# Moving the gate chunk, spreading the layer-norm statistics and regrouping the last branch gates in a two-layer encoder step

## The chip, the cores and the metric

The kernel runs on one core of a Trainium2 chip. The metric is the device time of one execution in microseconds. TensorE is called PE in the profile, VectorE DVE, ScalarE ACT, GpSimd POOL, SyncE SP.

## The reference

The model step has DEPTH = 2 layers over 512 prompt tokens and 64 sample tokens (576 columns together), D_MODEL 1024. What matters here is the first half of a layer:

```python
h = rms_norm(x, p['g_pre_mix']) * (1 + sc1) + sh1
mq, mk, mv, mo, mi, mf, su, sv, wq, wk, wv, gl = split_in(h @ p['w_in'])
ig = mi + b_igate;  lf = log_sigmoid(mf + b_fgate)          # 4 heads each: the gate rows
h_ml = mlstm_scan(q, k, v, ig, lf)                          # cumulative sums and maxima of lf, ig
y_ml = sigmoid(mo) * h_ml
y_sg, v_norm = spatial_gating(su, sv, ln_v_g, ln_v_b, ...)  # layer_norm(sv), then 128x128 mixing
y_sw = swa_prompt(rope(wq), rope(wk), wv, sinks)            # windowed attention
gates = sigmoid(gl).reshape(B, S, 3, D_MODEL)
merged = gates[0]*(y_ml @ w_br_mlstm) + gates[1]*(y_sg @ w_br_gmlp) + gates[2]*(y_sw @ w_br_swa)
x = x + g1 * rms_norm(merged @ p['w_out'], p['g_post_mix'])
```

A SwiGLU feed-forward part (hidden 2816) follows; the change leaves it alone.

## The kernel before

**Arithmetic and weights.** Activations lie with the features on the partitions and the 576 tokens in the free dimension. Each fp32 operand of a projection is split into a high part and a remainder (`h_hi`, `h_lo`; for a weight `hi`, `lo`), and three products are summed: hi·hi, hi·lo, lo·hi. A chunk is 128 output features: 8 k-tiles x 3 products x 2 halves of 288 columns = 48 matmuls (`feature_group`, L759; `main` calls it). SP loads a weight chunk into one of two RAW buffers (`load`, L576), POOL splits it with two instructions (`split`, L711 and L714) into one of two slots, of up to five where memory is free, PE uses it. All are numbered by position in the layer (P_QK = 0, ...), and each engine walks its own list of instructions, written out by hand, with semaphores between them. `carry` (L527) is a leading dummy (on PE a tiny matmul) that carries a wait.

**PSUM.** There are four units of two banks. Which unit a result gets follows from its place in the list ORDER, modulo four: a group may start once the group four places before it has been read (`empty`, `read`).

**Start of a layer.** `stream` takes the first chunks together, k-tile by k-tile, as `h_hi` and `h_lo` come (qk0 to qk2 in layer 0, qk0 to qk3 in layer 1); then come the remaining chunks up to qk7, then `wvif`, the token-major chunk of wv and the gate columns (L826, 120 matmuls of 136 columns), then `wk`. In layer 0 parts of the adaLN modulation stand between the chunks: `mod(0, a)` (L891, 64 PE instructions each), for which SP loads 2 MB of w_ada once the modulation two before it has freed its buffer (`ada_after`, L564); ScalarE copies it (L1402), PE transposes it back (`mback`, L900), VectorE takes it over (L1721).

**The gate rows.** After wk, PE transposes the gate columns into rows (`gt1`, L964, and `gt2`, L969). VectorE copies them (L1916 to L1920), and a chain of operations on 4 partitions x 576 follows, alternating between VectorE and ScalarE: -|f| (L1923), Exp and Ln (L1440, L1442), log-sigmoid (L1925), two cumulative sums (L1928), maxima (L1933, L1934), and last exponentials (L1444 to L1447, the last one writes `win` and sets `rows_ready`). PE meanwhile computes chunk v0 and then waits for `rows_ready` before `gt3` (L1062, L1064); v1 comes next.

**Attention slots and layer norm.** Ten attention slots are spread between the chunks sv0 to sv3 and the first branch. In slot i, PE does the output of slot i-2, the transposes of i-1 (L1168) and the scores of i (L1151); VectorE does `sw_max` (L2101 and after), then, for i = 4, `ln_stats` as the `between` work: bn_stats and bn_aggr of five token tiles (L2157, L2160) and two additions (L2162, L2163); then `sw_norm` once ScalarE's exponentials (L1561, L1563) are there, whose last multiplication writes `sm`. `ln_root` follows slot 5's merges; `ln_apply(t)` is the between work of slots 7 to 11. ScalarE takes the root between slots 5 and 6.

**Branches and merge.** For each branch b and each pair n of output tiles there are two gate chunks `g{b}_{n}` (ScalarE: tanh into TS) and one weight chunk for two branch groups `br{b}_{n}` of 24 matmuls each. VectorE merges (L2187 for b = 0; L2190 into WQ, then L1698 into MID for b = 1 and 2). After the last merge ScalarE writes `h_hi` of the eight tiles (L1631) and VectorE `h_lo` (L2222), and `stream` (L804 for the products with h_hi, L810 for those with h_lo) takes wo0 and wo1 together in the order k = 0 to 7. `p1` post-tiles follow.

Of the kernel before, what the change touches and what calls it, by code (L numbers as in the profile page):

```python
# [15 lines left out]
DEPTH, D, SEQ, DSEQ, PAST = 2, 1024, 512, 64, 128  # L16
# [27 lines left out]
def constants():  # L44
# [22 lines left out]
    for h in range(4):  # L67
# [16 lines left out]
AFTER = {0: {"qk3": (0, (5,), (4,)), "qk4": (0, (6,), (5,)), "qk5": (0, (7,), (6,)), "qk6": (0, (8,), (7,)),  # L84
# [28 lines left out]
def qk_order(l):  # L113
    out = [f"qk{i}" for i in range(STREAM[l])] + ([mod(0, 4)] if l == 0 else [])
    for i in range(STREAM[l], 8):
        out += [f"qk{i}"] + after(l, f"qk{i}")
    return out
# [11 lines left out]
MIX += ["gt1", "gt2", "v0", "gt3", "v1", "vt0", "kt0", "v2", "vt1", "cm0", "kt1", "v3", "vt2",  # L129
# [40 lines left out]
MIX += with_squares("wo", "p1")  # L170


def ffn_order(l):
    lm, (a, b) = IN_P1[l]
    out = [mod(lm, a), "p1s", "p1t", mod(lm, b), "p1b", "n2b"]
    for c, nb in enumerate(BLOCKS):
        for i in range(2 * nb):
            out += [f"fi{c}_{i}"] + after(l, f"fi{c}_{i}")
        if c == 1 and l == 0:
# [6 lines left out]
         for n in start_order(l) + qk_order(l) + ["wvif"] + after(l, "wvif") + ["wk"] + after(l, "wk") + MIX  # L186
# [6 lines left out]
P_QK, P_WVIF, P_WK, P_V, P_MO, P_WQ, P_SU, P_SV, P_BR = 0, 8, 9, 10, 14, 18, 22, 26, 30  # L193
# [7 lines left out]
CHUNK_OF.update({f"qk{i}": i for i in range(8)})  # L201
# [4 lines left out]
for _b_ in range(3):  # L206
    for _n in range(8):
        _p = P_BR + 12 * _b_ + 3 * (_n // 2)
        CHUNK_OF[f"g{_b_}_{_n}"] = _p + _n % 2
        if _n % 2:  # L210
            CHUNK_OF[f"br{_b_}_{_n}"] = _p + 2
CHUNK_OF.update({f"wo{i}": P_WO + i for i in range(8)})
# [58 lines left out]
def build(nc, A, O):  # L271
# [4 lines left out]
    with ctx:  # L276
# [176 lines left out]
        hl_ready = event("hl_ready", 24)  # L453
        nabs_ready = event("nabs_ready", 1)
# [96 lines left out]
        def _(sp):  # L551
# [6 lines left out]
            for l in range(DEPTH):  # L558
# [56 lines left out]
                if l == 0:  # L615
# [8 lines left out]
                    for i in range(5, 8):  # L624
                        cols(i % 2, i, w_in, i * 128)
                        ada_after(0, i + 1, i - 1)
                else:
                    for i in range(8):
                        cols(i % 2, i, w_in, i * 128)
# [3 lines left out]
                if l == 0:  # L633
                    ada_after(0, 9, 7)
                cols(1, P_WK, w_in, C_WK)
# [7 lines left out]
                for b, (nm, g, _) in enumerate(BRANCHES):  # L643
                    w_br = A[{"ml": "w_br_mlstm", "sg": "w_br_gmlp", "sw": "w_br_swa"}[nm]][ds(l, 1)] \
                        .rearrange("l (k p) c -> p (l k) c", p=128)
                    for q in range(0, 2):
                        for e in range(6):
# [3 lines left out]
                            else:  # L651
                                load(e % 2, pos, RAW[e % 2][:, 0:1024].rearrange("p (k c) -> p k c", k=4),
                                     w_br[:, :, ds(q * 512 + e // 3 * 256, 256)])
                w_out = A["w_out"][ds(l, 1)].rearrange("l (k p) c -> p (l k) c", p=128)
# [67 lines left out]
        def _(pe):  # L722
# [14 lines left out]
            for l in range(DEPTH):  # L737
# [56 lines left out]
                def stream(names, pos, ready, between=None):  # L794

                    for k in range(8):
# [1512 lines left out]
```

## Time and profile before

| what | value |
|---|---|
| three runs | 2290.62, 2290.75, 2292.04 us; median 2290.75 |
| profiled execution | 2293.98 us, its span 2292.2 us, mean granted PE clock 0.961 |
| PE, PEld busy | 2161.1 us (94%), 2080.6 us (91%) |
| DVE, ACT, POOL busy | 726.1 us (32%), 398.7 us (17%), 1237.5 us (54%) |
| DMA | 211 MB, mean 92 GB/s; the SP queue 31.9% of 16 engines' span |

The span is the time from the first to the last instruction of the profiled execution. Busy shares are averages over stages. "Released by" or "waited for" names what ended an idle stretch. PEclk is the granted TensorE clock as a share of 2.4 GHz. All times of a view are microseconds from the start of the span.

### The profile page before, as it was taken

To read this page: it belongs to the slowest core of one execution; us is meant where nothing else is said; L and a number is where in the kernel's file an instruction comes from. 1 tells how busy PE (TensorE), PEld (TensorE's weight loads), DVE (VectorE), ACT (ScalarE), POOL (GpSimd) and SP (SyncE) were. 2 spreads that over 40 slices of the span, in tenths; PEclk is the share of its full clock that TensorE was granted. 3 is DMA by queue.
4 is the path that set the end of the run, shared out by engine and by line. 5 is a ranking of instruction groups with operands and counts; after the bars stand their busy time and mean duration, and the time that the engine had idled before them with its cause. 6 is when DMAs were issued, how large, how long until landed. Compare 5 with 4: busy or idle time off the path is not lost.

```text
span 2292.2 us, 38070 instructions
## 1 busy us (share of the span) xinstructions
PE 2161.1 (94%) x16861; PEld 2080.6 (91%) x16861; DVE 726.1 (32%) x1201; ACT 398.7 (17%) x880; POOL 1237.5 (54%) x604
## 2 busy tenths in 40 slices
PE   4989999999999999999989799999999999999996
PEld 3889898999998999999989798989998899999996
DVE  4322366523255110011450335662324531001113
ACT  1211114211132110011221111330102211001111
POOL 2343353567762665666734444446686347667762
PEclk7899999999998999999979899999999899999998
DMA  8653421123342442442322152212233212222221
GB/s 267 227 166 38 65 75 56 56 77 92 93 157 64 148 145 71 125 148 75 92 56 56 47 65 62 69 47 76 76 100 127 77 49 81 73 84 83 81 76 60
DMA packets 319684, 211.05 MB, mean 92 GB/s; under 512 B 12528, under 2 KB 292512, under 8 KB 319392
## 3 DMA queue, kind: packets, MB, share of 16 engines
q1 hardware_dynamic: 312928, 205.13, 31.9%
q10 hardware_dynamic: 6592, 3.48, 0.6%
q8 instruction: 133, 2.18, 0.4%
q14 instruction: 31, 0.25, 0.0%
HBM read 203.80 MB, written 4.07 MB: 91 GB/s over the span
## 4 chain that ended last, share of the span: by engine, by line
PE 88%; DVE 5%; POOL 3%; ACT 1%; issue 1%; ACTq 1%; DMA 0%; SPq 0%; DVEq 0%; POOLq 0%
PE ps L759 59%; PE ps L784 10%; PE ps L804 4%; PE ps L891 2%; PE ps L810 2%; POOL lo L714 2%; POOL hi L711 1%; PE ps L844 1%; PE ps L826 1%; PE ps L1151 1%; PE ps L1022 1%; PE ps L1168 1%; PE ps L1192 1%; DVE h_lo L2222 1%; PE ps L1037 1%
## 5 line engine op out<-in xcount | busy, mean ns | idle before, releaser
L711 POOL TENSOR_TENSOR hi<-raw,consts 128x1024 fp32r<-128x1024 f32 (+3 forms) x260 | 467.2, 1797 | 902.8 <-PE ps L759 598.5
L714 POOL TENSOR_TENSOR lo<-raw,hi 128x1024 fp32r<-128x1024 f32 (+3 forms) x260 | 606.6, 2333 | 20.4
L759 PE MATMUL ps<-h_hi,hi 128*128 128x288 f32 x2720 | 591.0, 299 | 0.7 <-issue 0.7
L759 PE MATMUL ps<-h_hi,lo 128*128 128x288 f32 x2720 | 583.3, 296 | 0.0
L759 PE MATMUL ps<-h_lo,hi 128*128 128x288 f32 x2720 | 583.3, 296 | 0.0
L759 PEld LDWEIGHTS ps<-h_hi,hi 128*128 128x128 f32 x2720 | 438.3, 189 | 7.3 <-issue 5.3
L759 PEld LDWEIGHTS ps<-h_lo,hi 128*128 128x128 f32 x2720 | 439.3, 189 | 0.9 <-issue 0.9
L759 PEld LDWEIGHTS ps<-h_hi,lo 128*128 128x128 f32 x2720 | 439.3, 189 | 0.0
L1698 DVE TENSOR_TENSOR tmp<-sq,ps 128x576 f32<-128x576 f32 x44 | 33.1, 753 | 595.5 <-PE ps L759 573.3
L784 PE MATMUL ps<-y_hi,hi 128*128 128x288 f32 x616 | 134.7, 300 | 10.7 <-POOL lo L714 9.5
L784 PE MATMUL ps<-y_hi,lo 128*128 128x288 f32 x616 | 132.2, 296 | 0.0
L784 PE MATMUL ps<-y_lo,hi 128*128 128x288 f32 x616 | 132.0, 296 | 0.0
L1435 ACT ACTIVATE tmp<-ps 128x576 f32<-128x576 f32 x64 | 41.6, 650 | 414.5 <-PE ps L759 414.5
L784 PEld LDWEIGHTS ps<-y_hi,hi 128*128 128x128 f32 x616 | 98.7, 189 | 16.1 <-POOL lo L714 14.1
L784 PEld LDWEIGHTS ps<-y_hi,lo 128*128 128x128 f32 x616 | 99.4, 189 | 0.0
L784 PEld LDWEIGHTS ps<-y_lo,hi 128*128 128x128 f32 x616 | 99.4, 189 | 0.0
L711 POOL TENSOR_TENSOR hx<-raw,consts 128x1024 fp32r<-128x1024 f32 x29 | 55.9, 1929 | 39.6 <-DMA raw<-in_w_ffn_in 21.6
L1651 ACT ACTIVATE y_hi<-tmp 128x576 fp32r<-128x576 f32 x44 | 30.2, 686 | 267.6 <-DVE tmp L1698 267.6
L714 POOL TENSOR_TENSOR lx<-raw,hx 128x1024 fp32r<-128x1024 f32 x29 | 71.7, 2471 | 2.3
L759 PE MATMUL ps<-y_hi,hi 128*128 128x288 f32 x320 | 70.7, 303 | 0.0
L759 PE MATMUL ps<-h_hi,hx 128*128 128x288 f32 x320 | 69.4, 298 | 0.8 <-DVE ps L1798 0.8
L759 PE MATMUL ps<-y_lo,hi 128*128 128x288 f32 x320 | 68.9, 297 | 0.0
(313 smaller groups left out, 2891.2 us busy)
## 6 DMA issues: line engine op xcount, KB each, us to landing
raw<-in_w_in SPq DMA_DIRECT2D x108, 512.0 KB
ada<-in_w_ada SPq DMA_DIRECT2D x24, 2048.0 KB, 8.6
raw<-in_w_ffn_in SPq DMA_DIRECT2D x88, 512.0 KB
raw<-in_w_ffn_out SPq DMA_DIRECT2D x32, 384.0 KB
raw<-in_w_ffn_out SPq DMA_DIRECT2D x32, 320.0 KB
raw<-in_w_out SPq DMA_DIRECT2D x16, 512.0 KB
raw<-in_w_br_mlstm SPq DMA_DIRECT2D x8, 512.0 KB
raw<-in_w_br_swa SPq DMA_DIRECT2D x8, 512.0 KB
```

Source lines behind the costliest of these rows:

```text
L711: pool.tensor_tensor(hi, RAW[s][:, 0:size], ONES[:, 0:1].to_broadcast([128, size]), ALU.mult).then_inc(chunk_hi, 1)
L714: pool.tensor_tensor(lo, RAW[s][:, 0:size], hi.bitcast(f32), ALU.subtract).then_inc(chunk_split, 1)
L759: m = pe.matmul(o[:, h, :], a[:, k, c0:c0 + 128], mv(k, h), start=(k == 0 and begins), stop=(k == nk - 1 and a is wl))
L784: m = pe.matmul(o[:, h, :], a[:, k - k0, :], mv(k, h), start=(k == 0 and begins), stop=(k == nb - 1 and a is wl))
L804: pe.matmul(halves(l, nm)[:, h, :], a[:, k, :], HM[0](k, h), start=(k == 0 and a is wh), stop=False)
L810: m = pe.matmul(halves(l, nm)[:, h, :], wh[:, k, :], HM[1](k, h), start=False, stop=(k == 7))
L826: m = pe.matmul(unit(l, name)[:, c:c + w], st[:, k * T + t * 128:k * T + t * 128 + 128], mv[:, k, :], start=(k == 0 and begins), stop=(k = ...
L844: m = pe.matmul(unit(l, name)[:, c + t:c + t + 1], sq[:, t0:t0 + 128], ONES[:, 0:1], start=(begins and t == 0), stop=ends, skip_group_chec ...
L891: m = pe.matmul(unit(l, nm)[32 * x:32 * x + 32, 0:128], CS[:, k, :], wv[:, k, x * 128:(x + 1) * 128], start=(k == 0), stop=(k == 7))
L1435: act.activation(split2(dst), halves(l, name), func, scale=scale).then_inc(unit_of(l, name), 1)
L1651: act.activation(y_tile(False, i), TS[:, e, :], ACT.Copy).then_inc(gh_ready, 1)
L1698: return dve.tensor_tensor(out, a, b, op)
```

## The change

1. **Gate chunk.** `wvif` takes position 6, right behind qk5; qk6, qk7 and wk follow at 7, 8, 9. The gate transposes gt1 and gt2 stand right behind it, ahead of qk6, and wait for a new semaphore `if_ready`, set by VectorE once the gate columns have their bias; VectorE copies wv afterwards. In layer 0 the modulation parts keep their order. ScalarE copies qk6 and qk7 between the Ln and the last exponentials, and wk behind them. VectorE reads the modulation parts that belong to qk6, qk7 and wk after the gate chain.
2. **Statistics.** Tiles 0 and 1 in slot 4, tiles 2 and 3 in slot 5, tile 4 and the two additions in slot 6, the root in slot 7, `ln_apply(t)` in slot 8 + t. ScalarE's root stands after slot 6.
3. **Last gates and merged tiles.** g2_4 to g2_7 are computed together, then br2_4 to br2_7. Merges of branches 1 and 2 are made in place in PSUM, then added into MID (tiles 0 to 3 of branch 2, and branch 1) or left in PSUM (tiles 4 to 7 of branch 2). The tanh of g2_6 and g2_7 goes into SQ. The merged tiles are split and streamed in the order 0, 4, 1, 5, 2, 6, 3, 7; a PSUM unit of tiles 4 to 7 is free when its `h_lo` is made.

```diff
-    for i in range(STREAM[l], 8):
+        if i == 6:
+            out += ["wvif"] + after(l, "wvif") + ["gt1", "gt2"]
...
+        if (_b_, _n) == (2, 4):
+            MIX += [f"g2_{_i}" for _i in range(4, 8)] + [f"br2_{_i}" for _i in range(4, 8)]
+            break
...
+MERGED = (0, 4, 1, 5, 2, 6, 3, 7)
-P_QK, P_WVIF, P_WK, P_V, P_MO, P_WQ, P_SU, P_SV, P_BR = 0, 8, 9, 10, 14, 18, 22, 26, 30
+P_QK, P_WVIF, P_WK, P_V, P_MO, P_WQ, P_SU, P_SV, P_BR = 0, 6, 9, 10, 14, 18, 22, 26, 30
...
+                def gate_rows():
+                    pe.wait_ge(unit_of(l, "gt1"), empty(l, "gt1"))
+                    pe.wait_ge(if_ready, nth(if_ready, l))
...
                 for i in range(n, 8):
+                    if i == 6:
+                        pe.wait_ge(chunk_split, split_count(l, P_WVIF))
+                        token_group("wvif", P_WVIF, 136)
+                        parts_after("wvif")
+                        gate_rows()
+                        run_begins(nm, CHUNK_OF[nm])
+                    feature_group(nm, CHUNK_OF[nm], 8, 128, 0, *HM, lead=True)
...
+                for n in range(4, 8):
+                    main(f"g2_{n}", CHUNK_OF[f"g2_{n}"])
+                for n in (4, 6):
+                    branch(2, n, CHUNK_OF[f"br2_{n + 1}"])
+                stream(["wo0", "wo1"], P_WO, 8, order=MERGED)
...
+                for i in range(6):
+                    projected(i)
                 modulation_tiles("wvif")
-                tile("wk", KA[:, 0:T])
                 act.wait_ge(nabs_ready, nth(nabs_ready, l))
                 act.activation(LFT, WR, ACT.Exp).then_inc(act_step, step())
                 act.wait_ge(act_step, step.all())
                 act.activation(WR, LFT, ACT.Ln, bias=1.0).then_inc(sp_ready, 1)
+                projected(6)
+                projected(7)
                 act.wait_ge(m_ready, nth(m_ready, l))
...
+                tile("wk", KA[:, 0:T])
...
                 for n in range(8):
-                    act.wait_ge(merged2, before(merged2, l, n))
-                    tile(f"g2_{n}", TS[:, n % 2, :], ACT.Tanh, 0.5)
+                    if n < 6:
+                        act.wait_ge(merged2, before(merged2, l, n))
+                    tile(f"g2_{n}", TS[:, n % 2, :] if n < 6 else SQ[:, n - 6, :], ACT.Tanh, 0.5)
-                for k in range(8):
+                for k in MERGED:
                     act.wait_ge(merged2, nth(merged2, l, k))
+                    act.activation(split2(cols(HH, k)), split2(MID[:, k, :]) if k < 4 else halves(l, f"br2_{k}"),
+                                   ACT.Copy, scale=0.5).then_inc(hh_ready, 1)
...
+                for t0, t1, o in tiles:
                     m = tt(IFT[:, t0:t1, :], o[:, :, 128:136], BIF[:, :].unsqueeze(1).to_broadcast([128, t1 - t0, 8]),
                            ALU.add)
+                m.then_inc(if_ready, 1)
+                for t0, t1, o in tiles:
+                    m = dve.tensor_copy(VSW[:, t0:t1, :], o[:, :, 0:128])
...
-                    w = WQ[:, n % 2, :]
-                    dve.scalar_tensor_tensor(split2(w), s, 1.0, halves(l, nm), ALU.add, ALU.mult).then_inc(unit_of(l, nm), 1)
-                    ins = tt(m, m, split2(w), ALU.add)
+                    dve.scalar_tensor_tensor(o, s, 1.0, o, ALU.add, ALU.mult).then_inc(dve_step, step())
+                    if b == 2 and n >= 4:
+                        tt(o, o, m, ALU.add).then_inc(merged2, 1)
+                        return
+                    tt(m, o, m, ALU.add).then_inc(unit_of(l, nm), 1)
                     if b == 2:
+                        dve.wait_ge(unit_of(l, nm), read(l, nm))
+                        dve.memset(SCRATCH[:, 0:1], 0.0).then_inc(merged2, 1)
...
+                ln_work = {4: lambda: ln_stats((0, 1)), 5: lambda: ln_stats((2, 3)), 6: ln_var, 7: ln_root}
+                ln_work.update({8 + t: lambda t=t: ln_apply(t) for t in range(NTT + 1)})
...
                 def merged_lo(k):
...
+                    src = split2(MID[:, k, :]) if k < 4 else halves(l, f"br2_{k}")
+                    m = dve.scalar_tensor_tensor(split2(cols(HL, k)), src, 0.5, split2(cols(HH, k)).bitcast(f32),
+                                                 ALU.mult, ALU.subtract)
+                    m.then_inc(hl_ready, 1)
+                    if k >= 4:
+                        dve.wait_ge(hl_ready, nth(hl_ready, l, x))
+                        dve.memset(SCRATCH[:, 0:1], 0.0).then_inc(unit_of(l, f"br2_{k}"), 1)
+                for n in range(4):
                     merge(2, n)
                 dve.wait_ge(done_by("g2_7"), done(l, "g2_7"))
+                merged_lo(0)
+                for k in range(4):
+                    merge(2, k + 4)
+                    merged_lo(k + 4)
+                    if k < 3:
+                        merged_lo(k + 1)
```

On SP the loads follow the new positions: in layer 0 the order is chunk 5, w_ada 6, wvif, w_ada 7, qk6, w_ada 8, qk7, w_ada 9, wk, w_ada 10, w_ada 11.

## Rows read from the trace of the kernel before

**Rows 1.** The page: busy time, share of the span and instructions of TensorE.
```profile
PE 2161.1 (94%) x16861; PEld 2080.6 (91%) x16861; DVE 726.1 (32%) x1201; ACT 398.7 (17%) x880; POOL 1237.5 (54%) x604
```

**Rows 2.** Waits of PE, whole trace: us in total, times, longest us.
```profile
PE ps L527 <- ACT win L1447: 22.8, 2, 11.5
...
PE ps L1168 <- DVE sm L1698: 9.3, 2, 4.7
```

**Rows 3.** Chain of work, layer 1, around the gates: start us, us, what.
```profile
1249.75 13.35 PE ps L826 x120
...
1269.54 0.89 PE ps L964 x8
...
1289.11 1.53 PE ps L1062 x15
1290.64 1.71 PE ps L1064 x8
```

**Rows 4.** Windows: stretch, length, busy per engine, PEclk, DMA share, GB/s.
```profile
167.00:173.00 6.00, 0.00 (x0) 0.00 (x0) 5.79 (x12) 0.48 (x1) 1.69 (x1) 0.50 0.32 87
...
1866.00:1967.00 101.00, 101.00 (x760) 101.00 (x759) 15.98 (x19) 10.56 (x16) 69.84 (x32) 1.00 0.27 77
```

**Rows 5.** Chain of work over the whole trace, long pieces.
```profile
144.83 3.63 PE ps L891 x128
...
177.90 8.62 PE ps L759 x48
...
1292.34 7.88 PE ps L759 x48
1301.32 6.38 PE ps L759 x48
```

**Rows 6.** Timeline of DVE and ACT, layer 0, slots 3 and 4.
```profile
365.26 1.23 DVE L1698 TENSOR_TENSOR sm<-sm,mx 128x1024 f32<-128x1024 f32 x1
...
372.89 0.69 DVE L2157 BATCH_NORM_STATS2 bn<-v_tok 128x6 f32<-128x512 f32 x1
...
373.84 0.69 DVE L2157 BATCH_NORM_STATS2 bn<-v_tok 128x6 f32<-128x512 f32 x1
...
378.86 3.11 DVE L1698 TENSOR_TENSOR sm<-sm,mx 128x1024 f32<-128x1024 f32 x1
...
374.87 0.19 ACT L1563 ACTIVATE mx<-mx 128x4 f32<-128x4 f32 x1
```

**Rows 7.** Chain of work, layer 0, attention slots 4 and 5.
```profile
367.77 1.02 PE ps L1168 x8
...
382.11 1.94 PE ps L1168 x8
384.06 2.01 PE ps L1151 x8
386.06 7.13 PE ps L759 x48
```

**Rows 8.** Chain of work, layer 0, merged tiles and stream.
```profile
630.60 8.14 DVE h_lo L2222 x3
...
647.04 0.29 PE ps L810 x2
```

**Rows 9.** Timeline, layer 0, last merge: DVE, ACT, POOL.
```profile
628.13 0.75 DVE L2190 SCALAR_TENSOR_TENSOR wq<-tmp,ps 128x576 f32<-128x576 f32 x1 [1.37 <-PE ps L759]
...
630.71 0.68 ACT L1631 ACTIVATE h_hi<-mid 128x576 fp32r<-128x576 f32 x1 [3.23 <-DVE mid L1698]
...
628.17 1.89 POOL L711 TENSOR_TENSOR hx<-raw,consts 128x1024 fp32r<-128x1024 f32 x1 [2.03 <-PE ps L759]
```

**Rows 10.** Transfers into ada, 100 to 160 us: time to landing.
```profile
DMA to landing us min/median/max: 7.9/8.0/8.0
```

**Rows 11.** Lines 2222 and 2190, all instructions: duration ns min/median/max.
```profile
L2222 DVE SCALAR_TENSOR_TENSOR h_lo<-mid,h_hi x16: 744/746/2939, 630.6 to 1753.7; 128x576 fp32r<-128x576 f32 x16
...
L2190 DVE SCALAR_TENSOR_TENSOR wq<-tmp,ps x32: 740/754/755, 485.6 to 1740.6; 128x576 f32<-128x576 f32 x32
```

More of the change, by code:

```diff
@@ L185 @@
 ORDER = [(l, n) for l in range(DEPTH)
-         for n in start_order(l) + qk_order(l) + ["wvif"] + after(l, "wvif") + ["wk"] + after(l, "wk") + MIX
+         for n in start_order(l) + qk_order(l) + MIX
          + ffn_order(l)]
@@ L200 @@
 CHUNK_OF = {}
-CHUNK_OF.update({f"qk{i}": i for i in range(8)})
+CHUNK_OF.update({f"qk{i}": i + (i >= 6) for i in range(8)})
 CHUNK_OF.update({"wvif": P_WVIF, "wk": P_WK})
@@ L211 @@
             CHUNK_OF[f"br{_b_}_{_n}"] = _p + 2
+CHUNK_OF.update({f"g2_{_n}": P_BR + 26 + _n for _n in range(4, 8)})
+CHUNK_OF.update({"br2_5": P_BR + 34, "br2_7": P_BR + 35})
 CHUNK_OF.update({f"wo{i}": P_WO + i for i in range(8)})
@@ L792, in run_begins, with stream @@
                     carry(pe, l, name)
-                def stream(names, pos, ready, between=None):
-                    for k in range(8):
-                        pe.wait_ge(hh_ready, nth(hh_ready, l, ready + k))
+                def stream(names, pos, ready, between=None, order=range(8)):
+                    for x, k in enumerate(order):
+                        pe.wait_ge(hh_ready, nth(hh_ready, l, ready + x))
                         for e, nm in enumerate(names):
-                            if k == 0:
+                            if x == 0:
                                 run_begins(nm, pos + e)
@@ L956, in _ @@
                 main("wk", P_WK)
                 parts_after("wk")
-                pe.wait_ge(unit_of(l, "gt1"), empty(l, "gt1"))
-                if apart(l, "wvif", "gt1"):
-                    pe.wait_ge(unit_of(l, "wvif"), read(l, "wvif"))
-                for c, o in ((0, 0), (4, 512)):
-                    for t in range(NTT):
-                        m = pe.transpose(unit(l, "gt1")[0:4, o + t * 128:o + (t + 1) * 128], IFT[:, t, c:c + 4], IDN)
-                m.then_inc(done_by("gt1"), 1)
@@ L1255, in _ @@
                     branch(1, n, pos + 2)
-                for n in range(0, 8, 2):
+                for n in (0, 2):
                     pos = P_BR + 24 + 3 * (n // 2)
@@ L1262, in _ @@
                     branch(2, n, pos + 2)
-                stream(["wo0", "wo1"], P_WO, 8)
+                for n in range(4, 8):
+                    main(f"g2_{n}", CHUNK_OF[f"g2_{n}"])
+                for n in (4, 6):
+                    branch(2, n, CHUNK_OF[f"br2_{n + 1}"])
+                stream(["wo0", "wo1"], P_WO, 8, order=MERGED)
                 run_begins("wo2", P_WO + 2)
```

126 lines of the change are left out of this document (62 added, 64 removed), and 2 rows, old and new, of the table AFTER.

## The prediction

> **What bounds the kernel now.** I read the page first: TensorE is busy for 94% of the span [rows 1]. So the question for each edit is which idle stretch of TensorE it removes, and whether another engine can bring it back. Next I read the list of waits of PE over the whole trace. Two of its rows belong to the code that the diff touches, each once per layer [rows 2]: a leading dummy matmul that waits for `win` of ScalarE (22.8 us in two waits, the longer 11.5, so the other 11.3), and a transpose of the attention that waits for `sm` of VectorE (9.3 us in two, so 4.65 each). Then I followed the chain of work around each, and around the `stream` of wo0 and wo1, the third place that the diff touches.
>
> First stall, gates. In layer 1 the transposes of the gate rows end at 1270.43 (1269.54 + 0.89), and gt3, which needs what the long chain of small VectorE and ScalarE operations makes of them, starts its transposes at 1289.11: 18.7 us, while PE has only v0, 6.4 us, to do [rows 3]. The clock view shows a granted clock of 0.50 inside the stall [rows 4]: the lower of the two levels, 1.2 GHz. The work behind it pays too: v1 takes 8.62 us in layer 0 and 7.88 in layer 1, against 6.38 for a chunk of 48 matmuls at full clock [rows 5].
>
> Second stall, layer-norm statistics. VectorE starts five bn_stats at 372.89, between the maximum and the normalising of attention slot 4. ScalarE has the exponentials ready at 375.06 (374.87 + 0.19), but the normalising multiplication begins only at 378.86 and then takes 3.11 us, where an earlier slot's takes 1.23 [rows 6]. PE gets on at 382.11, and at the low level: eight transposes 1.94 us where the slot before shows 1.02, the scores 2.01, the branch groups 7.13 [rows 7].
>
> Third stall, merge to output projection. The stream of wo0 and wo1, 96 matmuls, ends at 647.33 (647.04 + 0.29) [rows 8]. The last branch group ended at 628.1: the merge that waits for it starts at 628.13 [rows 9]. That is 19.2 us for work that at 6.38 us per 48 matmuls takes 12.8, or 13.1 with its two leading dummies. The last merge comes first, then h_hi and h_lo of eight tiles; the first three h_lo take 8.14 us together, 2.7 each [rows 8].
>
> **The change part by part.** The profiled execution took 2293.98 us around a span of 2292.2; the median of three runs is 2290.75, 3.2 us less. The parts are sums of waits inside the span, so I take them off the median.
>
> *Gates.* PE's instructions are moved, not added, but for one dummy with its wait in layer 1. Behind wvif and the gate transposes PE now has qk6, qk7, wk and v0, four chunks or 25.5 us, before gt3 asks for the rows: 6.8 us more than the 18.7 of the chain, so the wait goes. Gained in layer 0: 11.3 of wait, 2.24 of v1 (8.62 - 6.38), and half of gt3's own 1.53 + 1.71, which is 1.6, since these lay at half clock [rows 2, 3, 5]; I bound that last item by 0 and 1.6 and take 1.6, because the nearest row, eight transposes at 1.94 against 1.02, halved too [rows 7]. Sum 15.1. Layer 1: 11.5 + 1.5 + 1.6 = 14.6. Price: the wait for `if_ready`. In layer 1 PE reaches it with nothing between (two small VectorE additions first, about 0.35 us) and the extra dummy costs 0.15; in layer 0 a modulation of 1.8 us covers it; 0.7 in all with handovers. **Gates: 29.0 us.**
>
> What queues behind the new waits: on ScalarE, qk6 and qk7 are copied between Ln and the last exponentials. The copy of qk7 is due 13 us after the transposes, before the rows it precedes; in layer 0 the modulation tiles 10 and 11 come there too, some 20 us after, so the rows come near 23 us, and PE asks for them near 33. wk's copy follows the rows and is needed by gt3 (layer 0) or vt0 (layer 1), later still. On VectorE the parts of modulation 8 to 11 now follow the gate chain, near 16.5 us; PE wants the unit of tile 8 for tile 9's way back after 19 us (0.4 + 0.2 + 6.4 + 1.8 + 0.3 + 6.4 + 3.6): 2.5 us to spare. On the SP queue load 11 waits for modulation 9, and its consumer now starts after qk7 and modulation 10, 6.4 + 1.8 + 0.4 = 8.6 us (two modulations take 3.63 [rows 5]); it lands 8.0 us after issue, in all four cases seen [rows 10]. Before, wvif's 13.35 us [rows 3] lay between, so this margin shrinks to about 0.5 us. On POOL, wvif's split is made two positions earlier; both slots rotate as before, and a split of about 4.3 us has the 13 us of wvif or the 6.4 of a chunk. All that is costed at nothing, by these covers.
>
> *Statistics.* A tile takes 0.95 us (one bn_stats at 372.89, the next at 373.84). Two of the five stay in slot 4 and end at 374.8, under ScalarE's exponentials that end at 375.06 [rows 6]. Slots 5 and 6 take 1.9 and 2.0, under equal exponentials. The normalising is then ready at 375.06 + 0.4 + 1.23 = 376.7, or 378.6 at the 3.11 of now; PE comes at 377.45 (382.11 less its wait). I take the first, as of the other slots. Gained: 9.3 of waits; the transposes 0.92 and the scores 0.95 per layer, 3.7; the branch groups 0.75 per layer, 1.5 [rows 2, 7]. ln_apply moves one slot on, its reader z0 is over 20 us away. **Statistics: 14.5 us.** The next thing late would be PE itself.
>
> *Last gate chunks and mixed order.* Let T be the end of g2_7. Before, 6.4 us of branch matmuls followed it; now 12.8, and the same total. The merges of tiles 4 to 7 come at T + 3.2, 6.4, 9.6, 12.8, and in the stream tile 4 stands second. What can be late now is a PSUM unit: br2_4 and br2_5 hold the units of wo0 and wo1 until their h_lo is made. No row shows a merge that stays in PSUM. Its nearest price is the merge from PSUM to SBUF, 0.75 us at 628.13 while POOL is at a split from 628.17 on [rows 9]; the upper bound is the longest h_lo, 2.94 [rows 11]. I take 0.75, because this row has the PSUM operand and POOL beside it. h_lo from SBUF (tiles 0 to 3) is 0.75 at its median and 2.7 in the first three [rows 8, 11]. Worst placing: h_lo 0 from T + 1.4 (tanh and h_hi first) to T + 4.1; merge 4 (1.5), h_hi (0.68 [rows 9]), h_lo 4 (0.75) to 7.1; h_lo 1 contended to 9.9; merge 5, h_hi 5, h_lo 5 to 13.0. PE asks for wo1's unit at T + 13.4 (12.8, a dummy and four matmuls). After that each k lasts 1.6 us: h_lo 7 is ready at T + 24.2 (13.0, twice 2.7 for h_lo 2 and 3, twice 2.9 for the rounds of 6 and 7) and due at 25.4. So nothing is late, even so. The stream falls from 19.2 to 13.1, **6.1 us in each layer, 12.2 in all**; bounds 0 and 6.5. The added memsets and the in-place merges of br1 lie beside over 12 us of matmuls before a unit is wanted again.
>
> On this point the row comes first: the h_lo of MID and h_hi took up to 2.94 us, the merge with one PSUM input never more than 0.755 in 32, and the one at 628.13 lay beside POOL [rows 9, 11]. The Trainium skill (SBUF — State Buffer, section Who interferes with whom) says that a VectorE instruction with two SBUF inputs contends with a GpSimd instruction that reads SBUF, and one with at most one SBUF input does not. By that rule the in-place merges and the h_lo of tiles 4 to 7 are safe and the total stays as I have it; by the upper bound taken for all operations alike it would be the first rival's upper end. The trace agrees for the forms it has.
>
> Sum: 29.0 + 14.5 + 12.2 = 55.7; 2290.75 - 55.7 = **2235.1 us**. A difference under about 0.2%, 4.6 us, could not be told from none.
>
> **The rivals.**
> 1. *The unit of wo1 becomes the new wait.* VectorE is behind in the last branch stretch, and PE waits at the stream's start. For it: 13.0 against 13.4 is thin, and each k needs VectorE. Against: the PSUM rows at 0.75 [rows 9, 11]. If it eats the third gain the time is 2290.75 - 43.5 = 2247. At its upper bound, all five operations of a round at 2.7, wo1 comes at T + 23.5, 10 us late in each layer plus 1.5 of low clock: 2247 + 2 x (11.7 - 6.1) = 2258. Chance 0.11, most of it near 2247.
> 2. *Layer 0 stalls at modulation 11 or at tile 9's way back.* A margin of 0.5 us against an unmixed 8.0 [rows 10], and 2.5 us against VectorE's chain. A stall of 3 us with 1.5 of low clock behind it: 2239. Chance 0.10.
> 3. *The gates' wait does not go*, because rows are now behind qk7's copy and its modulation tiles in ScalarE's order: it does not do what it says. Then only 26.7 are gained: 2264. Against: 23 us against 33. Chance 0.03.
> 4. *Slower: the clock.* The gaps removed are PE's only rest in the layers. If filling them made the chip hold PE below full clock elsewhere, the loss is over all 2161 us of PE time [rows 1]: 55.7 / 2161 = 2.6%, so below a mean of 0.961 / 1.026 = 0.937 (0.961 is the mean clock of the table of times) the change loses; at 0.92 it is 2235 + 2161 x (0.961/0.92 - 1) = 2331. Against: over 101 us of unbroken matmuls the clock stood at 1.00, and the low level is seen in the stall [rows 4]. Chance 0.03.
>
> **How the numbers follow.** The forecast keeps 0.73, with its own range 2230 to 2241 (gt3's half clock 0 to 1.6 twice, a stream that gives 5 to 6.5, handovers, the run's spread of 1.4). Rival 1, and rival 2 where its stall is longer, end above it, so the range reaches from 2229 to 2247: it leaves out rival 1's upper part, rivals 3 and 4. Every case but the fourth is faster by over 0.2%; that three gains all fail without loss has 0.01. Faster 0.96, same 0.01, slower 0.03.
>
> **What would show it.** In the list of waits: no row for `win`; none for `sm`; the wait of the stream's h_lo gone; a new row of some 0.3 us at the gate transposes for if_tok in layer 1. v1 at 6.4 us, gt3 near 1.7, the branch groups after slot 5 at 6.4, the stream at 13.1, PE busy near 94% rising to 96%, the clock up to about 0.98. Against me: a wait of the leading dummy of wo0 or wo1 for h_lo of L2222's successor or its memset (rival 1); a wait for ada or for mod in layer 0 (rival 2); PEclk under 1.00 inside long matmul runs (rival 4).

## The result and the profile after

The changed kernel takes 2240.77 us (median of four runs, 2239.13 to 2246.09) beside 2291.39 us for the kernel before (four runs): ratio 0.9783, 95% interval 0.9766 to 0.98. That is 50.6 us less, where 55.7 were forecast: faster, and 5.1 us short. The profiled execution is the slowest of the four, 2246.09 us; against the profiled execution of before (2293.98) it is 47.9 us less, and the stages below are taken from these two.

The page after, its busy times and the clock in 40 slices of the span:

```profile
PE 2151.9 (96%) x16863; PEld 2073.0 (92%) x16863; DVE 710.8 (32%) x1217; ACT 399.2 (18%) x880; POOL 1231.4 (55%) x604
...
PEclk7899999999998999999979999999999799999998
```

PE is busy 9 us less than in [rows 1]: matmuls that ran at the low clock now run at the high one. The rest of the gain is idle time. The list of waits of PE after the change, whole trace:

```profile
PE ps L1044 <- ACT mo_su L1465: 1.1, 1, 1.1
...
PE ps L970 <- DVE if_tok L1731: 0.4, 1, 0.4
...
PE ps L907 <- DMA ada<-in_w_ada: 0.4, 1, 0.4
```

The two rows of [rows 2], for `win` and for `sm`, are gone, and so is the wait of the stream for `h_lo` of the merged tiles. In their place stand two of 0.4 us: the gate rows of layer 1 wait for the biased gate columns, and modulation tile 11 in layer 0 waits for its matrix. The wait for `mo_su`, a gate tile of ScalarE, took 0.3 us before; it is taken up with the stores below. The longest waits that are left belong to the start, the norms and the feed-forward part, which the change leaves alone.

Now the three places. Gates, layer 1, the chain after the change (it answers to [rows 3]):

```profile
1226.02 0.27 DVE if_tok L1731 x2
...
1226.43 1.03 PE ps L970 x8
...
1227.97 25.96 PE ps L775 x192
...
1254.09 0.93 PE ps L1084 x15
1255.02 0.89 PE ps L1086 x8
1255.91 8.10 PE ps L775 x48
```

The gate transposes end at 1227.5, four chunks follow, and gt3 starts at 1254.09 without any wait. Its 23 small operations take 1.82 us (3.24 before). But v1, the 48 matmuls behind it, takes 8.10 us, where it took 7.88 behind the stall. Layer 0 shows the same:

```profile
138.61 9.14 DMA ada<-in_w_ada
...
163.15 0.93 PE ps L1084 x15
164.08 0.89 PE ps L1086 x8
164.97 8.09 PE ps L775 x48
```

The windows around it, columns: stretch, its length, busy times of PE, PEld, DVE, ACT and POOL, the granted clock, DMA share and GB/s:

```profile
163.00:165.00 2.00, 2.00 (x26) 1.97 (x26) 0.00 (x0) 0.65 (x1) 1.86 (x1) 0.97 0.51 150
165.00:168.00 3.00, 3.00 (x13) 3.00 (x14) 0.60 (x7) 0.00 (x0) 2.41 (x2) 0.50 0.00 0
168.00:170.00 2.00, 2.00 (x16) 2.00 (x16) 0.00 (x0) 0.00 (x0) 0.00 (x0) 0.92 0.71 193
```

PE is busy in every one of them, and the granted clock falls to 0.50 (1.2 GHz) right behind gt3 and returns some 3.5 us later.

Statistics, slot 4 of layer 0, VectorE's timeline and PE's chain (they answer to [rows 6, 7]):

```profile
359.94 0.69 DVE L2190 BATCH_NORM_STATS2 bn<-v_tok 128x6 f32<-128x512 f32 x1
...
362.55 1.23 DVE L1731 TENSOR_TENSOR sm<-sm,mx 128x1024 f32<-128x1024 f32 x1
```
```profile
364.50 1.02 PE ps L1190 x8
365.53 1.06 PE ps L1173 x8
366.59 6.57 PE ps L775 x48
```

Two tiles of statistics (the first is shown) lie under the exponentials, the normalising takes 1.23 us and ends at 363.78, and PE comes for it at 364.50, 0.7 us later. Transposes and scores are back at full clock.

Merge, layer 0, VectorE's timeline (it answers to [rows 8, 9]):

```profile
603.04 0.77 DVE L1731 TENSOR_TENSOR ps<-ps,mid 128x576 f32<-128x576 f32 x1
604.53 0.76 DVE L2265 SCALAR_TENSOR_TENSOR h_lo<-ps,h_hi 128x576 fp32r<-128x576 f32 x1 [0.72 <-ACT h_hi L1663]
605.33 1.85 DVE L2265 SCALAR_TENSOR_TENSOR h_lo<-mid,h_hi 128x576 fp32r<-128x576 f32 x1
...
610.17 2.96 DVE L2265 SCALAR_TENSOR_TENSOR h_lo<-mid,h_hi 128x576 fp32r<-128x576 f32 x1
```

Everything with an operand in PSUM takes 0.75 to 0.77 us, the `h_lo` of two SBUF operands up to 2.96. POOL's timeline fits the long ones: a split ran from 604.17 to 606.57, and the `h_lo` that began at 605.33 ended at 607.18; another split ran from 610.11 to 612.51, and the `h_lo` that began at 610.17 ended at 613.13. Each ended 0.6 us after the split did, while the `h_lo` from PSUM at 604.53, beside the first split, took 0.76. The unit of wo1 is free at 605.3, and PE asks for it at 608.85, 3.5 us later. The stream runs from 607.99 to 621.19, 13.2 us, without a wait.

The same pieces of the two chains of work, matched, give the account in us. Gates: 13.2 in layer 0 (15.1 less its share of the price were forecast) and 11.1 in layer 1 (14.6 less its share). Statistics: 7.1 and 7.3 (14.5 in all forecast). Merge: 6.09 and 6.09 (12.2 forecast). The sum, 50.9, is 3.0 more than the difference of the two executions. Most of that lies in stretches that the change hardly touches: from the end of the stream of layer 0 to the last weight split ahead of layer 1, and from the end of the stream of layer 1 to the end of the span, the changed kernel took 1.0 and 1.7 us more. The same two stretches vary from 573.9 to 576.3 us and from 531.0 to 535.8 us over the thirteen profiled executions of this document, and the kernel before happened to have 574.8 and 532.4.

### The profile page after: what moved, and what is told of

It reads as the page before. It is cut to its first block, busy times and chain, and to the rows that moved or that the text cites. A ratio compares the mean times of both kernels' runs of the same rounds, so it can differ in the third digit from the quotient of the medians.

```text
span 2244.3 us, 38092 instructions
## 1 busy us (share of the span) xinstructions
PE 2151.9 (96%) x16863; PEld 2073.0 (92%) x16863; DVE 710.8 (32%) x1217; ACT 399.2 (18%) x880; POOL 1231.4 (55%) x604
## 4 chain that ended last, share of the span: by engine, by line
PE 91%; POOL 3%; DVE 2%; ACT 1%; issue 1%; DMA 1%; ACTq 1%; SPq 0%; DVEq 0%; POOLq 0%
PE ps L775 61%; PE ps L800 10%; PE ps L820 4%; PE ps L907 2%; PE ps L826 2%; POOL lo L730 2%; POOL hi L727 1%; PE ps L860 1%; PE ps L842 1%; PE ps L1214 1%; PE ps L1044 1%; PE ps L1173 1%; PE ps L1190 1%; PE ps L1059 1%; PE ps L868 1%
## 5 line engine op out<-in xcount | busy, mean ns | idle before, releaser
L727 POOL TENSOR_TENSOR hi<-raw,consts 128x1024 fp32r<-128x1024 f32 (+2 forms) x260 | 467.1, 1797 | 861.2 <-PE ps L775 552.4
L730 POOL TENSOR_TENSOR lo<-raw,hi 128x1024 fp32r<-128x1024 f32 (+2 forms) x260 | 601.1, 2312 | 20.4
L775 PE MATMUL ps<-h_hi,hi 128*128 128x288 f32 x2752 | 597.6, 299 | 0.0
L775 PE MATMUL ps<-h_hi,lo 128*128 128x288 f32 x2752 | 590.4, 296 | 0.0
L775 PE MATMUL ps<-h_lo,hi 128*128 128x288 f32 x2752 | 589.9, 296 | 0.4 <-issue 0.4
L775 PEld LDWEIGHTS ps<-h_hi,hi 128*128 128x128 f32 x2752 | 443.4, 189 | 7.3 <-issue 5.3
L800 PE MATMUL ps<-y_hi,hi 128*128 128x288 f32 x616 | 134.8, 300 | 11.3 <-POOL lo L730 10.0
L800 PE MATMUL ps<-y_lo,hi 128*128 128x288 f32 x616 | 131.8, 296 | 0.0
L800 PEld LDWEIGHTS ps<-y_hi,hi 128*128 128x128 f32 x616 | 98.8, 189 | 16.6 <-POOL lo L730 14.6
L1465 ACT ACTIVATE sq<-ps 128x576 f32<-128x576 f32 x48 | 31.3, 652 | 229.7 <-PE ps L775 229.7
L775 PE MATMUL ps<-h_hi,hx 128*128 128x288 f32 x288 | 62.9, 300 | 0.8 <-DVE ps L1831 0.8
L775 PE MATMUL ps<-y_hi,hi 128*128 128x288 f32 x288 | 63.2, 301 | 0.0
```

What stands on the lines that cost most here:

```text
L727: pool.tensor_tensor(hi, RAW[s][:, 0:size], ONES[:, 0:1].to_broadcast([128, size]), ALU.mult).then_inc(chunk_hi, 1)
L730: pool.tensor_tensor(lo, RAW[s][:, 0:size], hi.bitcast(f32), ALU.subtract).then_inc(chunk_split, 1)
L775: m = pe.matmul(o[:, h, :], a[:, k, c0:c0 + 128], mv(k, h), start=(k == 0 and begins), stop=(k == nk - 1 and a is wl))
L800: m = pe.matmul(o[:, h, :], a[:, k - k0, :], mv(k, h), start=(k == 0 and begins), stop=(k == nb - 1 and a is wl))
L1465: act.activation(split2(dst), halves(l, name), func, scale=scale).then_inc(unit_of(l, name), 1)
```

## The experiments

They ran in three groups, each on one chip beside the kernel before: the three parts alone and `gt3_spread` (before 2294.05 us, eleven runs); `change_again`, `gt3_clumps`, `gt3_filler` and `merge_natural` (2294.1, nine runs); `gt3_clumps_2`, `gt3_middle` and `merge_sbuf` (2295.25, nine runs). Ratios are to the kernel before of the same group, and the median of a variant is over four to six executions.

### Each part alone

The edits are those of the diff: for `gates_alone` its first part (`P_WVIF` at 6, the gate rows ahead of qk6, the orders of loads, copies and parts that belong to it), for `stats_alone` the second, for `merge_alone` the third, on the kernel before. The core of `stats_alone`:

```diff
-                def ln_stats():
+                def ln_stats(tiles):
...
-                        slot(x, ln_stats if x == 4 else (lambda: ln_apply(x - 7)) if 7 <= x < 12 else None)
+                        slot(x, ln_work.get(x))
```

> Only the first part of the change (wvif and the gate transposes ahead of qk6); statistics and the last gate chunks as before. Theory (three independent stalls): the two waits for win go (22.8 us), gt3 runs at full clock (1.5 us per layer less), v1 stays near 8.1 us as in the changed kernel, so 24.5 to 26 us less than before. My forecast of the prediction: 29.0 less, with v1 at 6.4 us. Rival (the parts help each other, and alone the time comes back at a later wait): under 20 us less. The waits for sm (9.3) and for h_lo of the stream (about 8) are still there.

> Only the layer-norm statistics over three slots. Theory: the two waits for sm go, and the half clock behind them: 14.5 us less than before, the difference seen between 360 and 400 us of layer 0 is 7.1 to 7.3. Rival: normalising becomes late in slot 5 or 6, where statistics now stand too, and 2 to 5 us come back: 5 to 10 us less.

> Only the last four gate chunks together, the merges in PSUM and the mixed order. Theory: the stream of wo0 and wo1 goes from 19.2 to 13.1 us in each layer, 12.2 us less. Rival (the unit of wo1 or a merge is late): a wait of the leading dummies at the stream's start, 0 to 6 us less.

| kernel | median us | ratio, 95% interval | less than before |
|---|---|---|---|
| gates_alone | 2267.02 | 0.9883 [0.9864, 0.9902] | 27.0 |
| stats_alone | 2281.47 | 0.9943 [0.9927, 0.9959] | 12.6 |
| merge_alone | 2282.65 | 0.9949 [0.9934, 0.9964] | 11.4 |

The sum is 51.0, and the change as a whole gives 50.6: within what these times resolve, some 4 us for each part, the parts neither help nor hinder each other. The intervals hold the forecasts of 14.5 for the statistics and 12.2 for the merge, and also the 29.0 for the gates, so the times alone do not show what is missing there; the chain does. With the gates alone v1 takes 8.09 us in both layers, as in the whole change, so the missing part needs no meeting of two edits.

### Where v1's time went: gt3 spread, in clumps, in the middle, with filler

The forecast took v1's 8.62 and 7.88 us for an after-effect of the stall. The stall is gone and v1 is still at 8.1; that alone shows that removing the stall does not give the time back. The new theory: the clock falls behind gt3's run of tiny operations. `gt3_spread` lays gt3's operations (19 in the code, 23 in the trace) three by three between the steps of v1:

```diff
                         for a, mv, begins in ((wh, mh, True), (wh, ml, False), (wl, mh, False)):
...
+                        if each is not None:
+                            each(k)
```

> The changed kernel, but the 19 small operations of gt3 (15 transposes of 4 rows, 4 matmuls of one column) stand three by three between the k steps of v1 instead of in one run ahead of it. Theory (the clock falls because 1.8 us of tiny operations in a row follow each other, not because of a wait: in the changed kernel nothing waits there, yet v1 takes 8.1 us): PEclk stays 1.00 over v1, v1 with the small operations in it takes 6.4 + 1.8 = 8.2 us instead of 1.8 + 8.1 = 9.9, 3.4 us less than the changed kernel in both layers together. Rival A (the clock falls for another reason, such as time since the last fall, or VectorE and POOL): the low level appears near the same place all the same and the time is that of the changed kernel within 1 us. Rival B (the small operations stall the big ones between them): slower by 1 to 3 us.

Measured: 2245.79 us, ratio 0.9787 [0.9772, 0.9802]. The chain of layer 0 in this kernel:

```profile
162.67 0.98 PE ps L775 x6
163.65 0.27 PE ps L1091 x3
...
171.93 0.99 PE ps L775 x6
172.92 0.44 PE ps L1006 x4
```

The clock stands at 1.00 throughout, in both layers, so the first half of the theory holds here. But each step of six matmuls takes 0.98 us in place of 0.80, the small operations take 2.4 us in place of 1.82, and gt3 and v1 together take 10.25 us, against 9.90 in the change (163.15 to 173.05). The 3.4 us that were expected did not come, and the ratio is that of the change (0.9783) within the intervals. A place where small and large operations meet costs some 0.2 us, and eight of them eat what the clock gives.

So fewer meetings. `gt3_clumps` puts ten of them behind the second step and nine behind the fifth; `gt3_middle` puts all behind the fourth; `gt3_filler` leaves them ahead of v1, with six full-size matmuls between them whose product nobody reads. `change_again` is the change itself, for a comparison on the same chip. The edit of `gt3_clumps`, against `gt3_spread`:

```diff
-                    for kind, x, c, t in small[3 * k:3 * k + 3]:
+                    a, b = {1: (0, 10), 4: (10, 19)}.get(k, (0, 0))
+                    for kind, x, c, t in small[a:b]:
```

> The changed kernel as it is, once more, beside the variants of this call, so that they are compared on one chip. Expected: about 2241 us where the kernel before takes 2291, the ratio 0.9783 as before within 0.15%. In its profile: v1 takes 8.1 us in each layer though nothing waits ahead of it, the granted clock falls to 0.50 behind gt3's small operations, and the two short waits (modulation tile 11 on its matrix, layer 1's gate rows on the rows' inputs) show 0.4 us each or less.

> The changed kernel with gt3's small operations in two clumps inside v1, the first ten behind its second step and the last nine behind its fifth, in place of all of them ahead of it. In the changed kernel gt3 and v1 take 9.9 us together at a clock that falls to 0.50; spread three by three they took 10.25 us at the full clock, since each of eight steps came to 0.98 us instead of 0.80. If the clock falls only behind a long run of small operations, and if each place where small operations meet large ones costs a fixed 0.2 us, two clumps pay 0.4 us and keep the clock: 6.4 + 1.8 + 0.4 = 8.6 us, 1.3 us less in each layer, and the whole is 2 to 3 us shorter than the change. Rival: ten small operations let the clock fall as all did, then v1 stays at 8 us, and the whole is within 1 us of the change. Rival 2: the small operations themselves are dearer between the large ones, whatever their grouping, then the sum stays near 10 us at the full clock.

> The changed kernel with six matmuls of full size (288 columns each, into the part of gt3's PSUM unit that nobody reads) between gt3's small operations, two behind each group of five transposes, and their result thrown away. They are extra work of 6 x 0.12 = 0.7 us in each layer. If the clock falls because TensorE does nothing but small operations for 1.8 us, the fillers keep it at 1.00, v1 falls from 8.1 to 6.4 us, and each layer comes out about 1.0 us shorter in spite of the extra work (bounds: 0.2 us shorter if each of three meetings costs 0.2 us more, 1.0 without), the whole 0.5 to 2 us shorter. Rival: the clock's fall comes from something else (the work of the chunk before, or the time since it began), then v1 stays at 8.1 us and the whole is 1.5 to 2 us longer.

> The kernel with gt3's small operations in two clumps once more, to see whether its lead over the change holds. In its first run gt3 and v1 took 8.99 us together in place of 9.92 in layer 0 (0.93 less, at a clock of 1.00 throughout), but only 1.2 us of the change's time went, with intervals that overlap. Expected: 0 to 2 us shorter than the change's ratio, so a ratio near 0.977; the same two sums in the trace within 0.1 us. Rival: the gain is given back behind the chunk, where TensorE waits for ScalarE's gate tile (1.2 us in that run) and in the matmuls behind it, then the ratio is the change's or above.

> All of gt3's small operations in one run again, but behind the fourth step of v1 in place of ahead of its first. Theory: a run of 23 small operations takes the clock down wherever it stands, so the granted clock falls to 0.50 behind it, and the four steps of v1 that are left and what follows them take up to twice as long for some 4 us: gt3 and v1 together 9.4 to 10 us, the whole within 1.5 us of the change. Rival: the clock falls only where small operations follow the end of a chunk, then v1 and gt3 take 6.4 + 1.8 + 0.3 = 8.5 us at 1.00 and the whole is 2 to 3 us shorter.

| kernel | median us | ratio, 95% interval | gt3 and v1, layers 0 and 1 |
|---|---|---|---|
| change_again | 2241.17 | 0.9771 [0.9754, 0.9788] | 9.92, 9.93 |
| gt3_clumps | 2239.93 | 0.9764 [0.9749, 0.9779] | 8.84, 8.87 |
| gt3_clumps_2 | 2239.59 | 0.9758 [0.9744, 0.9771] | 8.84, 8.83 |
| gt3_middle | 2242.33 | 0.9771 [0.9756, 0.9785] | 8.52, 10.10 |
| gt3_filler | 2247.44 | 0.9799 [0.9783, 0.9814] | 10.07, 13.10 |

The chain of `gt3_clumps_2`, layer 0, the clock at 1.00 in all its windows:

```profile
160.99 1.77 PE ps L775 x12
162.76 0.65 PE ps L1092 x10
163.41 2.58 PE ps L775 x18
165.99 0.37 PE ps L1092 x5
166.36 0.89 PE ps L1094 x8
167.25 2.58 PE ps L775 x18
```

48 matmuls take 6.93 us here (1.77 + 2.58 + 2.58) instead of 8.1, and gt3 and v1 together 1.1 us less, in both layers of both profiles with the clumps. Two other kernels put a limit to the theory. `gt3_middle`, the chain of layer 1 and two of its windows:

```profile
1249.82 3.38 PE ps L775 x24
1253.19 0.93 PE ps L1092 x15
1254.12 0.89 PE ps L1094 x8
1255.02 4.90 PE ps L775 x24
```
```profile
1253.00:1255.00 2.00, 2.00 (x26) 1.86 (x24) 0.00 (x0) 0.00 (x0) 1.15 (x1) 1.00 0.04 8
1255.00:1258.00 3.00, 3.00 (x18) 3.00 (x18) 0.60 (x7) 0.00 (x0) 0.00 (x0) 0.69 0.66 175
```

In layer 1 the second half of v1 takes 4.90 us at a granted clock of 0.69 in its first 3 us and 0.61 in the next 2; in layer 0 of the same execution the same half took 3.32 at 1.00. With the filler the clock held in layer 0 (v1 6.60 us) and fell in layer 1 (v1 9.25 us). Neither of my two stories for `gt3_middle` came out: it is one in one layer and the other in the other.

The profiles of `merge_natural` and `merge_sbuf`, further down, have gt3 ahead of v1 just as the change has, and differ from it only later in the layer. `merge_sbuf`, the chain of layer 1 and a window:

```profile
1252.28 0.93 PE ps L1084 x15
1253.21 0.89 PE ps L1086 x8
1254.10 6.59 PE ps L775 x48
```
```profile
1254.00:1256.00 2.00, 2.00 (x16) 1.99 (x16) 0.60 (x7) 0.00 (x0) 1.92 (x2) 1.00 0.03 8
```

The same run of 23 tiny operations, and v1 takes 6.59 us at a clock of 1.00. It does so in both layers of `merge_sbuf` and in layer 0 of `merge_natural`; in layer 1 of `merge_natural`, in both executions of the change and in `gates_alone` v1 takes 8.09 or 8.10. So with gt3 ahead of v1 the clock fell in seven places of ten, in the middle in one of two, with the filler in one of two, in clumps in none of four and spread in none of two. That the tiny operations have to do with the fall is likely by these counts, and not shown: it comes in some executions of the same code and not in others, and what decides it stays open.

The counts also price the clumps. Where the clock holds, gt3 and v1 behind it take 8.41 us (1.82 + 6.59), and with the clumps 8.84, so the clumps cost 0.4 us; where it falls, they save 1.1. With a fall in seven places of ten that is 0.6 us for each layer, 1.2 in all, an estimate from these few places.

The whole of `gt3_clumps` came 1.2 us under the change on the same chip, and the second time its ratio was 0.9758. The intervals overlap with the change's, so that it is faster is likely and not shown by the times. Executions also differ further on, where ScalarE's queue issues the stores of the states. In `gt3_clumps_2`, the chain there:

```profile
213.93 2.73 issue
...
219.40 11.31 ACTq L1505
...
231.93 0.66 ACT mo_su L1476
```

A store of 4 bytes per partition held ScalarE's queue for 11.3 us, and the gate tile that PE needs behind it comes only when PE gets there. The same store took 11.76 us in the profiled execution of before, 12.56 in that of the change and 12.59 in that of `gt3_clumps`, and none took over 1.3 in `change_again`; PE's wait for the gate tile was 0.3, 1.1 and 1.2 us in the first three and under 0.2 in `gt3_clumps_2`. The 2.73 us in which PE stood still for nothing that the profile shows are another matter: `gt3_spread`, without a long store, has 2.6 at the same place, `gt3_middle` 1.3, `change_again` 0.5. Both come and go from one execution to the next.

The filler was wrong in its whole: 6.3 us slower than the change on its chip, where 0.5 to 2 us faster was expected. The chains show 3.3 of it, nearly all in layer 1 (13.10 against 9.93); where the rest lies is not shown.

### Order and place of the merged tiles

`merge_natural` splits and streams the merged tiles in the order 0 to 7, `merge_sbuf` keeps the mixed order and makes the last four merges in SBUF again.

```diff
-MERGED = (0, 4, 1, 5, 2, 6, 3, 7)
+MERGED = tuple(range(8))
...
-                    merged_lo(k + 4)
                     if k < 3:
                         merged_lo(k + 1)
+                for k in range(4, 8):
+                    merged_lo(k)
```

> The changed kernel with the merged tiles split and streamed in the order 0 to 7 in place of 0, 4, 1, 5, 2, 6, 3, 7; all else stays (merges of tiles 4 to 7 in PSUM, last four gate chunks together). The two output chunks then begin in the units of merged tiles 4 and 5, whose low parts come only behind the merges of all four tiles. From the changed kernel's timeline: low part 0 ends at 597.9, then three more low parts from SBUF of 1.9 to 3.0 us and four merges of 1.5 us each bring the low part of tile 4 to about 611.5, where the stream asks for the unit at 608.0. So TensorE waits about 3.5 us for the unit of tile 4 (bounds 1.5 if the low parts from SBUF take 1.3, 6 if they take 3.0), once in each layer: 7 us slower than the change in all, 3 to 12. Rival: the mixed order is worth nothing, since the units come free in time or the stream then runs without other waits: within 1 us of the change.

Measured: 2252.31 us, ratio 0.9822 [0.9806, 0.9839], 11.1 us slower than the change on the same chip. The list of waits has the predicted row, and the chain shows what follows it:

```profile
PE ps L536 <- DVE scratch L2270: 5.2, 2, 2.6
```
```profile
607.70 1.26 PE ps L820 x4
...
610.41 0.86 PE ps L826 x4
```

PE waits 2.6 us in each layer for the unit that the low part of tile 4 sets free, and the matmuls behind the wait run at the low clock: in layer 0 the first two groups of the stream take 1.26 us each where the change has 0.71, in layer 1 the loss comes a group later. Matched against `change_again`, the stretch costs 3.8 us in layer 0 and 4.2 in layer 1; the other 3 us of the 11.1 are not traced. So the mixed order carries about 8 of the 12.2 us of this part: computing four gate chunks together is worth little unless the tile whose unit is wanted first is split early.

The core of the edit of `merge_sbuf`, against the change:

```diff
+                    if b == 2 and n >= 4:
+                        w = split2(WQ[:, n % 2, :])
+                        dve.scalar_tensor_tensor(w, s, 1.0, o, ALU.add, ALU.mult).then_inc(unit_of(l, nm), 1)
+                        dve.wait_ge(unit_of(l, nm), read(l, nm))
+                        tt(m, m, w, ALU.add).then_inc(merged2, 1)
+                        return
...
-                    if b == 2 and n >= 4:
-                        tt(o, o, m, ALU.add).then_inc(merged2, 1)
-                        return
```

> The changed kernel with the merges of tiles 4 to 7 of the last branch made in SBUF as before the change (the product with the gate into a work tile, the sum of two SBUF tiles into the merged tile, the high and low parts read from there); the order of gates, splits and the stream stays. In the changed kernel a low part from PSUM takes 0.76 us beside a running split of POOL, and one from SBUF up to 2.96. If VectorE and POOL hinder each other on two SBUF operands, each of the four sums and four low parts that move to SBUF takes 1.5 to 2.9 us beside POOL's splits in place of 0.77: about 10 us more work of VectorE between 598 and 616 us, of which TensorE, whose stream has some 3 us in hand, sees 3 to 6 us in each layer: 6 to 12 us slower than the change. Rival: the gain of the merge part comes from the order alone (the last four gate chunks together), and the place of the sums costs nothing: within 1.5 us of the change.

Measured: 2245.3 us, ratio 0.9785 [0.9772, 0.9799]; the interval overlaps with those of the change, so the times alone do not show a loss. The chain before its stream's last step:

```profile
617.00 0.77 DVE mid L1731
...
617.79 0.69 ACT h_hi L1663
...
618.52 1.32 PE ps L820 x8
```

and the grouped operations of VectorE in `change_again` and in this kernel:

```profile
L2265 DVE SCALAR_TENSOR_TENSOR h_lo<-mid,h_hi 128x576 fp32r<-128x576 f32 x8 | 13.7, 1711 | 50.6 <-ACT h_hi L1663 50.4
L2265 DVE SCALAR_TENSOR_TENSOR h_lo<-ps,h_hi 128x576 fp32r<-128x576 f32 x8 | 6.1, 758 | 5.7 <-ACT h_hi L1663 5.7
```
```profile
L2268 DVE SCALAR_TENSOR_TENSOR h_lo<-mid,h_hi 128x576 fp32r<-128x576 f32 x16 | 26.5, 1685 | 56.4 <-ACT h_hi L1663 56.4
L1731 DVE TENSOR_TENSOR mid<-mid,wq 128x576 f32<-128x576 f32 x8 | 12.1, 1511 | 0.3
```

Two SBUF operands cost 1.69 us on average for a low part and 1.51 for a sum; one in PSUM costs 0.76. The mechanism is as expected, but the size is not: VectorE is late only twice in each layer, with the low part of tile 6 (PE waits 0.8 us) and the high part of tile 7 (0.5), and the matched chain loses 2.1 and 2.0 us, 4.1 in all, where 6 to 12 were expected. I had taken 3 us for what the stream has in hand; my reading is that it had more, since a step of the stream lasts 1.6 us and each gives VectorE more time. The Trainium skill (SBUF — State Buffer, section Who interferes with whom) states that the pair of ports which VectorE uses for a second SBUF operand is shared with GpSimd and locked by one at a time. By that rule the in-place merge is worth the difference of these rows, and the rows agree with it.

## Why the prediction was right, and what was off

The sign, the three parts and nearly all of their covers came out as worked; the range (2229 to 2247) holds the result, which lies at the upper end of the main case's own range (2230 to 2241). Step by step:

- **Statistics, 14.5.** Right: 7.1 and 7.3 by the matched chains (the branch groups came to 6.57 us, as in the other slots, and not to 6.38), and the margin of PE behind the normalising was 0.75 us by the working and 0.7 in the trace.
- **Last gate chunks, 12.2.** Right in the sum: 6.09 in each layer, the stream 13.2 us. The price of the in-place merge, taken as 0.75 from the one row with a PSUM operand beside POOL, is 0.76 and 0.77. The first rival (the unit of wo1) did not come; it was drawn with 0.4 us in hand at worst and the trace has 3.5, because the low parts of tiles 0 and 1 took 1.29 and 0.75 us there, where 2.7 and 2.8 were put in. That another order of the low parts brings it is shown by `merge_natural`.
- **Gates, 29.0.** The waits of 11.3 and 11.5 us went, and gt3 itself is at full clock, with 1.4 us gained in each layer (3.24 to 1.82) where 1.6 were taken. The step that failed is "2.24 of v1 (8.62 - 6.38)" in layer 0 and the 1.5 of layer 1. I read v1's length as the price of the stall ahead of it. In the change it takes 8.09 and 8.10 us with no idle time of PE ahead: 0.53 saved in layer 0 and 0.22 lost in layer 1, so 3.4 of the 3.7 us are missing. What stands in its place is a fall of the clock with PE busy, which comes in seven of the ten places with gt3 ahead of v1 and not in the other three (v1 6.59). Whether the stall or gt3 held the clock down for v1 in the kernel before, where it took 8.62 and 7.88, no run separates: none has the stall and gt3 in another order.
- **The price of the new waits.** 0.4 us for the gate columns in layer 1, as taken (0.35). The second rival came in small: the margin of modulation 11 was put at 0.5 us by a landing of 8.0 us, the transfer took 9.1, and PE waited 0.4. The landing time was the number to doubt: 8.0 was the longest of [rows 10], which cover 60 us of the trace, while the page of the kernel before gives 8.6 as the median of all 24 such transfers, as long as the whole cover.
- **Clock.** The fourth rival (the clock held down by fewer rests) is refuted: the mean rose from 0.961 to 0.968 in the profiled execution, to 0.971 in the other three and to 0.970 to 0.973 in `change_again`. The 0.98 that the prediction named as a sign was not reached.
- **What remains of the 5.1 us.** Beside v1's 3.4, gt3 gave 0.4 us less than taken and modulation 11 took 0.4. The other 0.9 us cannot be placed. The profiled execution of the change has 1.2 us more at the low clock in layer 1: 288 matmuls beside the gates took 41.29 us (15.33 + 25.96), where before 240 of them took 33.73 and the hidden chunk at full clock 6.4. But in `change_again` the same 288 took 40.12 (14.49 + 25.63), so that belongs to the execution and not to the change.
- **The first rival's upper end.** With the rival's own terms (1.4 us, eight operations of VectorE at 2.7 and two `h_hi` of 0.68 until the unit is free) it comes at T + 24.4 and not at T + 23.5, 2 us more in the whole; nothing rests on it, since that part lay outside the range and did not come.

Of single executions one has to know that the start alone differs by over 3 us: the same step of the first stream begins at 65.09 in `change_again` and at 68.88 in the profiled execution of the change, at a lower clock before it. Stages must be matched piece by piece, and ends not compared.

## What to carry to other kernels

A slow stretch behind a stall need not come back with the stall: look at what stands between them. When PE is busy and its clock is still low, ask what sort of instructions ran last, and look at the same place in several executions before giving it a cause; here two profiles of the change agreed, and three more places with the same code did not. Small operations in two clumps between large matmuls kept the clock here, at 0.4 us; one by one they cost more than they gave. When results are consumed in the order in which their buffers come free, make that order part of the design: here it carried two thirds of a regrouping's gain. And take the margin of a matrix's transfer from all its landings in the trace, not from those of one stretch.

## What the runs showed that I had not expected

- Behind a run of 23 tiny operations (the transposes and matmuls of gt3), 1.8 us without any idle time, the granted clock fell to 0.50 for about 3.5 us in seven of ten places, and stayed at 1.00 in three; with the same operations in two clumps it stayed at 1.00 in all four places.
- Between small operations six matmuls of 288 columns take 0.98 us in place of 0.80.
- One store of 4 bytes per partition, issued by ScalarE's queue, took at most 1.3 us in one execution of the change and 12.56 in another.
- VectorE's operations in place in PSUM, 128 x 576, cost 0.75 to 0.77 us (a product in 32 places, a sum in 8), also beside a split of POOL, while a low part of two SBUF operands ended 0.6 us after the split that it ran beside.
